# A two-stream encoder kernel: score matmuls issued in pairs, the gate projected one unit ahead, and other numbers in its scheduler

## The reference

```python
# layer 0: 16 query heads of 64, 4 key/value heads, each query block of 128 sees 3 key blocks
s = einsum(q, k) * scale;  p = exp(s - m);  o = (p / (sum(p) + exp(sink - m))) @ v;  mix = o @ w_o
# layer 1
b_gate, c_gate, xv = split(h @ w_in)
mix = (b_gate * _dwconv3(c_gate * xv, conv_w)) @ w_out
# after both mixers
g, u = split(h @ w_gate_up)                          # 2 x 2816 columns
f = (silu(_dwconv3(g, conv_w)) * u) @ w_down
# around every part: h = h + rmsnorm(part(rmsnorm(h)))
```

## Time and profile before

| | |
|---|---|
| median of three runs | 3266.52 us |
| the profiled execution, its own time | 3258.35 us |
| its span, from the first to the last instruction of the slowest core (5) | 3256.8 us |
| spans of the other cores | 3226.8 to 3255.1 us |
| PE busy | 3046.3 us, 94% |
| DVE, ACT busy | 1877.8 us (58%), 1858.3 us (57%) |
| PE's share of the chain that ended last | 79% |
| mean granted PE clock, core 5 | 0.975 of full speed |

### The profile page before, as it was taken

One profiled execution on the slowest core, in us unless ns is written; L12 is line 12 of the kernel. 1 busy time (PEld: TensorE's weight loads), 2 busy tenths in 40 slices (PEclk: granted clock), 3 DMA queues, 4 the chain that ended last, 5 costly groups with the idle time before them and its releaser, 6 DMA issues.

```text
span 3256.8 us, 52570 instructions; the slowest of 8 cores (3226.8 to 3256.8 us)
## 1 busy us (share of the span) xinstructions
PE 3046.3 (94%) x14950; PEld 1434.2 (44%) x14950; DVE 1877.8 (58%) x3611; ACT 1858.3 (57%) x3624; POOL 410.2 (13%) x771
## 2 busy tenths in 40 slices
PE   4889989998999899999999999999999999999997
PEld 1323434343443344433444344434444357646565
DVE  6656633656635663567753676366763566366753
ACT  4775545455457653376556665565745776445752
POOL 1001111112112201111011101111001220120101
PEclk9889999999999999999999999999999999999998
DMA  6358998989986756747576657556655665666556
GB/s 136 110 152 207 203 238 219 206 221 224 228 211 184 235 169 184 213 149 200 168 203 178 183 172 206 176 162 184 175 153 157 181 187 163 184 189 188 163 165 170
DMA packets 306266, 602.31 MB, mean 185 GB/s; under 512 B 39234, under 2 KB 65090, under 8 KB 305986
## 3 DMA queue, kind: packets, MB, share of 16 engines
q1 hardware_dynamic: 238466, 421.68, 44.1%
q0 software_dynamic: 67520, 177.26, 23.4%
HBM read 530.89 MB, written 116.13 MB: 199 GB/s over the span
## 4 chain that ended last, share of the span: by engine, by line
PE 79%; DMA 10%; ACT 3%; issue 3%; DVE 3%; SPq 1%; POOL 0%; DVEq 0%; ACTq 0%; POOLq 0%
PE ps L355 79%; DMA gc<-hd 2%; DMA w<-bgu 1%; DMA w<-wgu 1%; DVE x_ L368 1%; DMA bgu<-w 1%; ACT rec L364 1%; DMA cst_sb<-cst 1%; SPq L390 1%; DMA w<-bd 1%; ACT pt L364 1%; DVE gc L378 1%; DMA w<-wd 1%; DMA xs<-xT 0%; ACT L364 0%
## 5 line engine op out<-in xcount | busy, mean ns | idle before, releaser
L355 PE MATMUL ps<-x_,w 128*128 128x512 bf16 (+6 forms) x8064 | 1665.0, 359 | 77.3 <-DVE act_ L368 33.5
L355 PEld LDWEIGHTS ps<-x_,w 128*128 128x128 bf16 x8064 | 783.8, 98 | 875.3 <-issue 152.7
L355 PE MATMUL ps<-act_,w 128*128 128x512 bf16 (+6 forms) x3744 | 812.1, 356 | 16.9 <-DMA w<-wd 6.8
L378 DVE SCALAR_TENSOR_TENSOR gc<-gs,cst_sb,gc 128x512 f32<-128x512 f32 (+10 forms) x1018 | 656.1, 652 | 158.1 <-ACT gc L364 113.5
L355 PEld LDWEIGHTS ps<-act_,w 128*128 128x128 bf16 x3744 | 355.2, 98 | 373.2 <-issue 56.8
L364 ACT ACTIVATE gs<-ps 128x512 f32<-128x512 f32 (+4 forms) x396 | 215.7, 548 | 390.0 <-PE ps L355 388.4
L364 ACT ACTIVATE gc<-gs,cst_sb 128x512 f32<-128x512 f32 (+6 forms) x468 | 312.5, 672 | 84.6 <-DVE gs L368 58.5
L368 DVE TENSOR_TENSOR act_<-act_,ps 128x512 bf16<-128x512 bf16 (+5 forms) x396 | 246.1, 626 | 164.6 <-ACT act_ L364 82.9
L364 ACT ACTIVATE act_<-gc 128x512 bf16<-128x512 f32 (+5 forms) x396 | 227.8, 579 | 182.5 <-DVE gc L378 171.3
L364 ACT ACTIVATE sq<-ps 128x512 bf16<-128x512 f32 (+7 forms) x288 | 158.0, 548 | 264.0 <-PE ps L355 262.9
L364 ACT ACTIVATE pt<-ps 128x512 bf16<-128x512 f32 x368 | 210.7, 597 | 91.3 <-PE ps L355 88.9
(11 more groups left out here) (94 smaller groups left out, 2235.1 us busy)
## 6 DMA issues: line engine op xcount, KB each, us to landing
w<-bgu SPq DMA_DIRECT2D x616, 256.0 KB, 3.5
w<-bd SPq DMA_DIRECT2D x224, 256.0 KB, 3.5
w<-bin SPq DMA_DIRECT2D x168, 256.0 KB, 3.2
hd<-x_ POOLq DMA_DIRECT2D x128, 256.0 KB, 5.5
w<-wgu POOLq DMA_DIRECT2D x88, 256.0 KB, 6.9
bgu<-w SPq DMA_DIRECT2D x88, 256.0 KB, 6.3
w<-bd SPq DMA_DIRECT2D x112, 192.0 KB, 3.3
gs<-hd POOLq DMA_DIRECT2D x68, 256.0 KB, 5.8
```

The source lines that it names most:

```text
L355: return lambda e: e.matmul(out, lhsT=lhsT, rhs=rhs, start=start, stop=stop)
L378: return lambda e: e.scalar_tensor_tensor(out=out, in0=in0, scalar=scalar, in1=in1, op0=o0, op1=o1)
```

## The change

Five edits. (1) `f_pair` makes one schedule entry of the two score matmuls: they stand next to each other on PE, wait for both banks, and are assumed to take 0.45 in place of 0.109 each. The entry has no bank on record, so `keep_busy` puts no dummies ahead of it. (2) The products with `v` count as ready 0.7 later (`g.slack`). (3) In `ffn` the gate of unit j+1, with its convolution and silu, is recorded ahead of the up half of unit j. (4) `conv_layer` is turned round likewise: the x and c projections of the next unit come ahead of the b projection of this one. (5) The norm work is due 45 later, not 30. The arithmetic is the same.

```diff
+def f_pair(a, b):
+    def both(e):
+        a(e)
+        return b(e)
+    return both
...
                         for hf in range(2):
                             lo = hf * 64
-                            mm(bks[hf].ap[:, :], k_t[tk % 3][lo:lo + 64, np_, (kb % 4) * 128:(kb % 4) * 128 + 128],
-                               qs[:, :, b * 128:(b + 1) * 128], True, True,
-                               [kB[tk % 3][np_], qB[t % 2][2 * np_ + hf][b]], bks[hf].buf, 256)
+                            ends.append(f_mm(bks[hf].ap[:, :],
+                                             k_t[tk % 3][lo:lo + 64, np_, (kb % 4) * 128:(kb % 4) * 128 + 128],
+                                             qs[:, :, b * 128:(b + 1) * 128], True, True))
+                            reads += [kB[tk % 3][np_], qB[t % 2][2 * np_ + hf][b]]
+                        op(PE, f_pair(*ends), 0.45, reads, [bks[0].buf, bks[1].buf])
...
+                        g.slack += 0.7
                         for ii, (tk, kb, pair) in enumerate(pts):
                             mm(od.ap[:, :], v_t[tk % 3][:, (kb % 4) * 4 + n, :], pair[hf].ap[:, :], ii == 0, False,
                                [vB[tk % 3][kb % 4], pair[hf].buf], od.buf, 512)
+                        g.slack -= 0.7
...
-            g.vt += 30.0
+            g.vt += 45.0
...
-            for j in range(NFF):
-                sg = load_w(...); su = load_w(...)
-                for ge in ges:
-                    gb = proj(sg, ge, False)
...
-                    ub = proj(su, ge, True)
-                    y = conv3(...)
...
-                yield 16 * t_mm(512)
+            units = [(j, ge) for j in range(NFF) for ge in ges]
+            def gate(j, ge):      # load, proj, edge_in, copy to gs, conv3, silu
...
+            def up(j, ge):        # load, proj, multiply into act, free the bank
...
+            gate(*units[0])
+            for i, unit in enumerate(units):
+                if i + 1 < len(units):
+                    gate(*units[i + 1])
+                up(*unit)
+                if unit[1] is ges[-1]:
+                    yield 16 * t_mm(512)
...
+            # conv_layer: gated(next unit) = x and c projections, product, conv3; out_gate(unit) = b projection, product
```

More of the change, by code:

```diff
@@ L789, in a_att @@
                         bks = [spool.get() for _ in range(2)]
+                        ends, reads = [], []
                         for hf in range(2):
@@ L1026, in ffn @@
             ges = [Geo(st, sub, si, lag) for si, sub in enumerate(subs)]
-            for j in range(NFF):
-                sg = load_w(st.w, ("gu", l, 2 * j), bgu[l, 2 * j], wgu[l, 2 * j], 1024)
-                su = load_w(st.w, ("gu", l, 2 * j + 1), bgu[l, 2 * j + 1], wgu[l, 2 * j + 1], 1024)
-                for ge in ges:
-                    gb = proj(sg, ge, False)
[L1032 to L1035, removed]
-                    ub = proj(su, ge, True)
[L1037 to L1043, removed]
-                yield 16 * t_mm(512)
@@ new lines, in ffn @@
+            units = [(j, ge) for j in range(NFF) for ge in ges]
+            slots = {}
+            def gate(j, ge):
+                if ge is ges[0]:
+                    slots["g"] = load_w(st.w, ("gu", l, 2 * j), bgu[l, 2 * j], wgu[l, 2 * j], 1024)
+                gb = proj(slots["g"], ge, False)
+                gs = st.gs.next()
+                edge_in(ge, gs, l * NFF + j)
+                op(ACT, f_act(gs.ap[:, 2:2 + ge.n], gb.ap[:, 0:ge.n], AF.Copy), t_act(ge.n), [gb.buf], [gs.buf])
+                st.pool.put(gb)
+                y = conv3(ge, gs, l * NFF + j,
+                          lambda jj, j=j: cst[:, C_FCW + (l * 3 + jj) * 22 + j:C_FCW + (l * 3 + jj) * 22 + j + 1])
+                silus[t, l] = op(ACT, f_act(st.act[:, j, ge.c0:ge.c0 + ge.na], y.ap[:, 0:ge.na], AF.Silu), t_act(ge.na),
+                                 [y.buf], st.acells(j, ge.c0, ge.c0 + ge.na), tab="silu")
@@ new lines, in up @@
+            def up(j, ge):
+                if ge is ges[0]:
+                    slots["u"] = load_w(st.w, ("gu", l, 2 * j + 1), bgu[l, 2 * j + 1], wgu[l, 2 * j + 1], 1024)
+                ub = proj(slots["u"], ge, True)
+                av, ab = st.act[:, j, ge.c0:ge.c0 + ge.na], st.acells(j, ge.c0, ge.c0 + ge.na)
+                op(DVE, f_tt(av, av, ub.ap[:, 0:ge.na], ALU.mult), t_dve(ge.na), ab + [ub.buf], ab)
+                st.pool.put(ub)
+            gate(*units[0])
[5 more added lines that the diff above has]
+                    yield 16 * t_mm(512)
@@ L1058, in conv_layer @@
             xi = 0
[L1059 to L1082, removed]
@@ new lines, in conv_layer, with gated @@
+            units = [(m, ge) for m in range(8) for ge in ges]
+            slots, ys = {}, {}
+            turn = [0]
+            def gated(m, ge):
+                if ge is ges[0]:
+                    slots["x"] = load_w(st.w, ("in", 16 + m), bin_[16 + m], win[16 + m], 1024)
+                    slots["c"] = load_w(st.w, ("in", 8 + m), bin_[8 + m], win[8 + m], 1024)
+                n = ge.n
+                xb = proj(slots["x"], ge, False)
+                xrow = 8 + 2 * (turn[0] % 3)
+                turn[0] += 1
+                xsv = st.act[:, xrow:xrow + 2, :].rearrange("p a b -> p (a b)").bitcast(F32)[:, 0:n]
+                xsb = st.actB[xrow] + st.actB[xrow + 1]
+                op(ACT, f_act(xsv, xb.ap[:, 0:n], AF.Copy), t_act(n), [xb.buf], xsb)
+                st.pool.put(xb)
+                cb = proj(slots["c"], ge, False)
+                cx = st.gs.next()
+                edge_in(ge, cx, 44 + m)
+                op(DVE, f_tt(cx.ap[:, 2:2 + n], cb.ap[:, 0:n], xsv, ALU.mult), t_dve(n), [cb.buf] + xsb, [cx.buf])
+                st.pool.put(cb)
+                ys[m, ge.si] = conv3(ge, cx, 44 + m, lambda jj, m=m: cst[:, C_CW + jj * 8 + m:C_CW + jj * 8 + m + 1])
@@ new lines, in out_gate @@
+            def out_gate(m, ge):
+                if ge is ges[0]:
+                    slots["b"] = load_w(st.w, ("in", m), bin_[m], win[m], 1024)
+                bb = proj(slots["b"], ge, True)
+                y = ys[m, ge.si]
+                op(DVE, f_tt(st.act[:, m, ge.c0:ge.c0 + ge.na], y.ap[:, 0:ge.na], bb.ap[:, 0:ge.na], ALU.mult),
+                   t_dve(ge.na), [y.buf, bb.buf], st.acells(m, ge.c0, ge.c0 + ge.na))
+                st.pool.put(bb)
+            gated(*units[0])
+            for i, unit in enumerate(units):
+                if i + 1 < len(units):
+                    gated(*units[i + 1])
+                out_gate(*unit)
+                if unit[1] is ges[-1]:
+                    yield 24 * t_mm(512)
```

## The result

The changed kernel took 3226.64 us in the median of four runs; its ratio to the kernel before is 0.9864, interval 0.9837 to 0.9890, so it is 1.1 to 1.6% faster. The forecast was 3209 us; the profiled execution took 3226.20 us, 32.15 less than that of before, where 57 were forecast.

A forecast was written before the change was run, and what follows sets the result against it. PE's own queue was taken to bound the kernel past 300 us. Terms -45 + 0 - 5 - 25 - 5 + 5 + 18 = -57 us gave 3201, plus 8.2 to the median 3209 us; range 3170 to 3240.

The forecast's parts named there:

- What bounds: Past 300 us PE's own queue sets the time; less PE work or waiting shortens the span, faster ACT or DVE does not.
- Edit 1, scores in pairs: Attention scores on PE: 114 fewer passages into and out of half-array work at 0.41 us each; -45 us.
- The pair's wait: Both banks must be free before either score starts; projections between pairs cover the second exponential; 0 us, bounds -20 to +30.
- Edit 2: Attention's products with `v`, placed later in the queue, fill waits for `pt`; -5 us, bounds -8 to +10.
- Edits 3 and 4: Gate ahead leaves 1.73 us more before an up half's bank is reused, so most `act_` waits go; -25 us.
- The clock: Fewer waits for the MLP's product mean fewer PE matmuls at the lower clock level; -5 us, bounds -20 to 0.
- Edit 5: Norm chain yields longer to the other stream's operations, so PE waits more for it; +5 us, bounds 0 to +60.
- slower: the norms: Rival: both streams' norms fall together and leave PE without work; 3298 us at 3 us each; chance 0.09.
- The late attention: Third round, tile 5: attention ends later and ACT's table changes outlast PE's work; +18 us, bounds 0 to +40.
- Sum: All terms over the whole kernel: -57 us on the profiled execution's 3258.35 us, giving 3201, or 3209 as median.
- The signs: Right: scores' busy time about 75 us, `act_` waits below 12, 96 table loads; wrong: PE idle past 300 us above 140.
- ACT bounds the attention: Rival: early pairs give nothing, late ones 39, waits take back 30, MLP's waits give 15; about 3242 us; chance 0.08.

The follow-up runs named there:

- the split: The changed kernel with its queues kept, but the next matmul put between the two scores in 151 pairs; ratio to the kernel before 1.004.

## Why the prediction was right, point by point

- **What bounds.** PE's queue past 300 us: right. The passages and steps given back by the split lengthened the time by 57 us (the profiled span by 46) for 151 x 0.41 = 62.
- **Edit 1, scores in pairs.** -45 forecast, -52.0 in the scores' busy time, -41.0 of it past 300 us. That two scores side by side cost what one does is right, and shown by the split and by edit 1 alone. That the 0.41 us is all passage, "not the score", is not: the run of four puts some 0.22 on the step and 0.19 on the passage. The count stands, since joining two lone scores saves both. The early passages gave nothing here, as forecast (16 us of PE's time became idle, 852 and 853 matmuls), but not for the reason given, that PE idles there anyway: with edit 1 alone 892 matmuls start in the first 300 us, 884 in its repeat.
- **The pair's wait.** 0 forecast, with bounds of -20 to +30; the scores' waits rose by 27.7 us (27.4 to 55.1). Of these, 16.3 lie in the first 300 us, most of them there without pairs too (23.6 us with all edits but the pairs). Past 300 us the term was mis-sized: 0 forecast, +11.4 measured, and +13.7 with edit 1 alone. "Projections stand between two pairs, which cover the second exponential" was true of the place shown and not of all: the bank that a pair needs is also that of the products with `v`, which comes free only after two reciprocals and a product on two busy queues. Past 300 us the waits for that product rose from 9.3 to 21.6 us, while those for exponentials fell from 8.8 to 5.7. I had priced the exponentials' banks alone.
- **Edit 2.** -5 forecast, -8.1 at the products with `v`, and yet two pairs of runs that differ in this edit alone make it 22 and 24 us slower, give or take 17 each, where +10 was the bound. The step that failed is to take a wait that goes for time that goes: in the first 300 us it came back at the scores, and the 900th matmul starts 11 us later with edit 2 in both pairs of runs. Where the rest of the 22 to 24 us arises stays open.
- **Edits 3 and 4.** -25 forecast, -16.8 measured, and -15.0 in the run of these edits alone. Of the 18.3 us left, 9.7 lie between 1740 and 1940 us, beside the late attention (4.2 before). Without edits 2 and 5 the waits were 9.6 us, 25.5 less than before, as forecast, and without edit 1 8.3. So the extra room can give what was forecast, and the order that the other edits make decides how much of it is seen; by what, is not shown.
- **The clock.** -5 forecast. PE's busy time past 300 us fell by 8.5 us beyond the scores' 41.0; how much of that is fewer matmuls at the lower level was not separated.
- **Edit 5.** +5 forecast, +5.2 in the waits for the norm (6.5 to 11.7), and no effect on the time in two comparisons. The rival "slower: the norms" needed 62 us there and is out.
- **The late attention.** +18 forecast. From 1740 to 1940 us PE's idle time rose by 15.1 us, but 6.3 of them are waits of scores and 5.5 waits for the MLP's product, so this term and the two above overlap, and the sum counted them as apart. The table loads came out as the queue had them, 96. Neither edit 1 nor edit 5 can be named as the cause: the stretch has 16.0 us of idle time with edit 1 alone, 19.4 with the others alone, 25.5 with all.
- **Sum.** -57 forecast, -32.2 in the span. PE's work came out as forecast: -45 - 5 = -50, and -49.5 past 300 us. The waits did not: 0 - 5 - 25 + 5 + 18 = -7 forecast, +17.3 measured. Past 300 us they are +11.4 at the scores, +2.7 at the products with `v` (3.6 to 6.3), -14.7 for the MLP's product (33.0 to 18.3), +5.2 for the norm and +12.7 elsewhere, 8.4 of them for ACT's `x_` (3.1 to 11.5). That the time still lies in the forecast's own range is owed to the work, which is the larger part; the waits were 24 us off.
- **The signs.** The scores' busy time (76.4), the starts of the two scores (less than 0.02 us apart in all 184 pairs), the 96 table loads and the new wait for `q` in the third round came; the waits for `act_` stayed above 12 us (18.3). Of the signs of being wrong one came true: PE's idle time past 300 us is 157.5 us, above the 140.
- The rival "ACT bounds the attention" was nearer than its chance of 0.08: its -24 us is 3242, the forecast 3209, the time 3226.64. Its terms come out almost as it had them: the early pairs give nothing, the late ones 41.0 (39), the MLP's waits 14.7 (15), and the other waits take back 32.0 (30); it lacks only the 8.5 us of other PE work. That ACT is what bounds is not shown: the exponentials kept their duration, 596 ns, and of these waits the one for DVE's product `q` rose most. The Trainium skill (TensorEngine Tiling (Array Packing), Performance Considerations, PSUM Bottleneck) says that tiling speeds up TensorE but not the emptying of PSUM, which may become the bottleneck after a speedup of 4; here two scores run at once. By that rule, the trace agrees in part: past 300 us the scores wait 12.3 us more for the banks that `q` empties and 3.1 less for those that the exponentials empty, and the pair at 1424.43 waits for neither.

## What to carry to other kernels

Matmuls that use half of the array are cheap only side by side: read the cost of a lone one and of a pair from the starts of their neighbours, count both in the queue, and multiply. When two operations are tied into one, list every holder of every buffer that the pair now needs at once, not only the one the loop shows. Read waits by stretch, and not in total, and count beside them how much work is done by then: an edit can move a wait and not remove it. In a kernel with a greedy schedule an edit that shortens one wait can still cost time, as edit 2 did: time each edit against the kernel without it.

## What the runs showed that I had not expected

Counting the pairs as ready 0.7 later put 52 more table loads on ACT, 148 in place of 96 at 1283 ns each, and cost some 33 us: one scheduling number for PE set the table changes of ACT. Among the kernels with pairs and the gate ahead, more table loads mostly went with a longer time: 86 loads 0.9805 and 0.9817, 92 loads 0.9797, 96 loads 0.9864 and 0.9866, 104 loads 0.9905, 106 loads 0.9878, 148 loads 0.9966. No run changes the loads alone, so that they are the cause is not shown. And edits 1, 3 and 4 alone are 60 to 64 us faster than the kernel before: the kernel without edits 2 and 5 has the -57 that was forecast for all five.
